# Two-layer hybrid attention and PEER kernel: rows summed twelve items late, query steps beside the lookups, the row's multiply ahead of the dense step

## What is computed

```python
q = (xc @ wq).reshape(P_CHUNK, P_HEADS, 2, P_HALF)
sc = jnp.einsum('thcd,hcnd->thcn', q, sub_keys)
s1, i1 = lax.top_k(sc[:, :, 0], P_TOPK)
s2, i2 = lax.top_k(sc[:, :, 1], P_TOPK)
# all 16 x 16 sums; the best 16 give top_s and eidx
...
gate = jax.nn.softmax(top_s, axis=-1)
u = jnp.take(u_tab, eidx, axis=0)
act = jax.nn.gelu(jnp.einsum('thkd,td->thk', u, xc))
vv = jnp.take(v_tab, eidx, axis=0)
return jnp.einsum('thk,thkd->td', gate * act, vv)
```

## Time and profile before

| | us |
|---|---|
| median of 3 runs | 3077.9 |
| lowest and highest run | 3075.38, 3078.37 |
| span of the profiled execution | 2949.8 |
| the median less that span | 128.1 |

### The profile page before, as it was taken

The page is one execution under the profiler, slowest core; times in us unless marked ns, Lnnn a source line. Parts: engine busy times, 40 slices in busy tenths (PEclk is TensorE's granted clock), DMA queues, the critical chain, the costliest instruction groups (busy, mean ns, idle before and its releaser), DMA issues.

```text
span 2949.8 us, 21918 instructions
## 1 busy us (share of the span) xinstructions
PE 1521.5 (52%) x6476; PEld 665.0 (23%) x6476; DVE 1618.3 (55%) x3970; ACT 280.5 (10%) x732; POOL 1562.8 (53%) x1601
## 2 busy tenths in 40 slices
PE   6677677677235523334445585776723333233344
PEld 2353235244001101111222133533500000000001
DVE  1427776454766556455641298655386675766510
ACT  0220023011000000001000002311100000000000
POOL 0006411376676556455566573126667777777765
PEclk9798775788557765566678896578866666556667
DMA  8669973699999989788899995248999999999988
GB/s 291 250 210 355 388 287 107 214 348 380 400 401 371 401 314 346 289 299 308 336 400 352 357 368 195 64 157 321 376 358 384 403 392 390 393 403 383 390 339 345
DMA packets 299015, 963.25 MB, mean 327 GB/s; under 512 B 28280, under 2 KB 30712, under 8 KB 298128
## 3 DMA queue, kind: packets, MB, share of 16 engines
q0 software_dynamic: 221184, 805.40, 71.4%
q1 hardware_dynamic: 77712, 156.44, 14.6%
HBM read 959.12 MB, written 2.62 MB: 326 GB/s over the span
## 4 chain that ended last, share of the span: by engine, by line
DMA 25%; PE 24%; DVE 17%; POOL 16%; issue 15%; ACT 1%; POOLq 0%; SPq 0%; DVEq 0%; ACTq 0%
DMA ring<-peer_v,v_rows 17%; POOL ring L670 16%; PE ps_acc L931 8%; DVE ring L1464 7%; DMA ring<-peer_u,u_rows 4%; PE ps_mm L754 3%; PE ps_mm L808 3%; DMA weights<-ada_w 2%; PE ps_mm L869 2%; DMA weights<-w_in 1%; PE ps_mb L834 1%; PE ps_acc L713 1%; PE ps_mm L897 1%; PE ps_tr L819 1%; PE ps_mb L693 1%
## 5 line engine op out<-in xcount | busy, mean ns | idle before, releaser
L931 PE MATMUL ps_acc<-ring,coef_cols 128*32 128x512 f32 x3072 | 603.9, 927 | 1137.7 <-DMA ring<-peer_v,v_rows 1137.7
L670 POOL DMA_INDIRECT ring<-peer_u,u_rows x768 | 785.9, 1023 | 668.2 <-DVE dots L1464 448.3
L670 POOL DMA_INDIRECT ring<-peer_v,v_rows x768 | 752.5, 980 | 444.6 <-issue 224.1
L1464 DVE CUSTOM_DVE_ANT_0 ring<-ring,ps_tr 128x1024 f32<-128x1024 f32 x512 | 616.3, 1220 | 330.0 <-DMA ring<-peer_u,u_rows 311.6
L931 PEld LDWEIGHTS ps_acc<-ring,coef_cols 128*32 128x32 f32 x3072 | 121.7, 145 | 1542.2 <-issue 1541.1
L1464 DVE CUSTOM_DVE_ANT_0 ring<-ring,h 128x1024 f32<-128x1024 f32 x256 | 307.7, 1224 | 111.7 <-DMA ring<-peer_u,u_rows 97.4
L754 PE MATMUL ps_mm<-weights,hT 128*128 128x512 f32 x480 | 218.1, 614 | 25.6 <-DMA weights<-w_in 21.1
L897 PE MATMUL ps_mm<-hT,weights 128*128 128x128 f32 (+1 forms) x1024 | 192.5, 345 | 3.6 <-issue 3.0
L897 PEld LDWEIGHTS ps_mm<-hT,weights 128*128 128x128 f32 x1024 | 164.3, 203 | 61.6 <-issue 48.0
L635 POOL TENSOR_SCALAR u_rows<-picks 128x16 uint32<-128x16 f32 x48 | 17.7, 368 | 230.8 <-DVE picks L1437 229.8
L1488 DVE TENSOR_TENSOR h<-h,ps_acc 128x1024 f32<-128x1024 f32 x6 | 7.3, 1221 | 224.3 <-PE ps_acc L931 224.3
(11 more groups left out here) (206 smaller groups left out, 1522.8 us busy)
## 6 DMA issues: line engine op xcount, KB each, us to landing
weights<-ada_w SPq DMA_DIRECT2D x24, 2048.0 KB, 9.9
weights<-w_in SPq DMA_DIRECT2D x20, 2048.0 KB, 14.3
weights<-peer_wq SPq DMA_DIRECT2D x16, 2048.0 KB, 13.8
weights<-w_out SPq DMA_DIRECT2D x8, 2048.0 KB, 15.6
ring<-peer_u,u_rows POOLq DMA_INDIRECT x768, 6.3
ring<-peer_v,v_rows POOLq DMA_INDIRECT x768, 6.4
weights<-peer_keys SPq DMA_DIRECT2D x4, 1024.0 KB, 6.5
par<-params SPq DMA_DIRECT2D x2, 1026.0 KB, 7.4
```

The lines of the kernel that those rows point to most:

```text
L670: pool.indirect_dma_start(ring[:, place % RING, :], None, src, bass.IndirectOffsetOnAxis(ap=rows, axis=0)).then_inc(row_full[place % RING] ...
L931: last = pe.matmul(ps_acc[QROWS * k:QROWS * (k + 1), b * NB:(b + 1) * NB], coef_cols[:, i // PART % 2, at:at + QROWS], ring[:, slot("v", n ...
L1464: dve.tensor_tensor_reduce(row, row, h, 1.0, 0.0, ALU.mult, ALU.add, dots[:, n // UNIT % 2, n % UNIT:n % UNIT + 1]).then_inc(u_used, 1)
```

## The change

It has four parts.

1. LAG is 12 instead of 8: TensorE adds v rows i - 15 to i - 12 at item i, and the last 12 behind the segment. ScalarE's third and fourth spread move from items 25 and 41 to 29 and 45. The order of lookups and the ring stay as they are.
2. Stages are cut into pieces. Of both stages of layer 0 and of the sample stage of layer 1 the first 5 pq steps stay with the stage, and 11 move beside the next lookups: the prompt's of layer 0 into unit 0 (weight 6 each), the sample's into the first 40 items of unit 2, those of layer 1 into the first 40 of unit 8. The prompt stage of layer 1 is as before. In layer 0 the sample stage's first 36 steps (through the 12th head of the first tile) go with unit 0, the rest up to the cut with unit 1; in layer 1 all up to the cut is spread evenly over units 6 and 7.
3. `route` waits for the two score copies of its own head instead of the stage's VectorE program waiting for all. The score matmuls of the sample stages go to `ps_mb` instead of `ps_tr`, and `hold_rows` no longer waits for the scores.
4. In an item with a u row VectorE makes its piece of the search, the gates and the multiply first, and the dense steps after them.

Cut to what differs:

```diff
-LAG = 8
+LAG = 12
...
+FIRST_PQ = 2 * AHEAD + 1
+def split_at(tiles):
+    return len(steps(tiles)) - 16 + FIRST_PQ
...
 class Beside:
-    def __init__(self, program, weights, weight, items):
-        self.program, self.weights, self.weight, self.share = program, weights, weight, weight / items
+    def __init__(self, pieces, programs, items):
+        self.steps = [(programs[piece.stage], weight) for piece in pieces for weight in piece.weights]
+        self.share = sum(weight for _, weight in self.steps) / items
...
     def item(self):
         self.due += self.share
-        while self.done < self.due - 1e-6 and self.done < self.weight:
-            self.done += self.weights[next(self.program)]
+        while self.at < len(self.steps) and self.done < self.due - 1e-6:
+            self.step()
...
+def pieces(name):
...
+    if name == "start":
+        return (Piece(P0, 0, split_at(P_TILES)),), 1
+    if name == "s0_first":
+        return (Piece(P0, split_at(P_TILES), None, 6), Piece(S0, 0, S0_HALF)), UNIT
+    if name == "s0_last":
+        return (Piece(S0, S0_HALF, split_at(S_TILES)),), UNIT
+    if name == "s0_rest":
+        return (Piece(S0, split_at(S_TILES)),), REST_ITEMS
+    if name == "p1":
+        return (Piece(P1),), 3 * UNIT + 20
+    if name == "s1":
+        return (Piece(S1, 0, split_at(S_TILES)),), 2 * UNIT
+    return (Piece(S1, split_at(S_TILES)),), REST_ITEMS
...
-    return (Segment(0, None, s0), Segment(1, 0, s0, True),
-            Segment(2, 1), Segment(3, 2, p1), Segment(4, 3, p1), Segment(5, 4, p1), Segment(None, 5, p1, True),
-            Segment(6, None, s1), Segment(7, 6, s1, True),
-            Segment(8, 7), Segment(9, 8), Segment(10, 9), Segment(11, 10), Segment(None, 11))
-SPREADS = {(0, S_TILES): 2 * UNIT, (1, P_TILES): 3 * UNIT + 20, (1, S_TILES): 2 * UNIT}
+    return (Segment(0, None, "s0_first", True), Segment(1, 0, "s0_last", True), Segment(2, 1, "s0_rest", True),
+            Segment(3, 2, "p1"), Segment(4, 3, "p1"), Segment(5, 4, "p1"), Segment(None, 5, "p1", True),
+            Segment(6, None, "s1"), Segment(7, 6, "s1", True), Segment(8, 7, "s1_rest", True),
+            Segment(9, 8), Segment(10, 9), Segment(11, 10), Segment(None, 11))
+REST_ITEMS = 40
+S0_HALF = 36
...
         def key_scores_at(l, tiles, i, n):
-            return ps_mb[:, (i % 2) * NB:(i % 2) * NB + n] if tight(l, tiles) else tr(i, n)
+            return tr(i, n) if (l, tiles) == P0 else ps_mb[:, (i % 2) * NB:(i % 2) * NB + n]
...
             def hold_rows(tau):
                 act.wait_ge(u_used, 2 * tau * UNIT)
-                act.wait_ge(ps_ready, group_nth(tau // T, S_TILES, 15, 16))
                 act.wait_ge(h_ready, nth(tau // T, S_TILES, 2, 2 * len(S_TILES) - 1))
...
                 for i in range(16):
                     yield "pq"
-                dve.wait_ge(ps_ready, group_nth(l, tiles, 15, 16))
...
             def route(n):
...
+                tiles = S_TILES if tau % T else P_TILES
+                dve.wait_ge(ps_ready, group_nth(tau // T, tiles, 2 * h + 1, 16))
                 dve.sem_inc(search_may, 1)
...
-                    side.item()
                     if g.u is None:
+                        side.item()
                         continue
...
                     dot(g.u * UNIT + i)
+                    side.item()
```

More of the change, by code:

```diff
@@ L129, in before_search, with __init__, step @@
         self.engine.sem_inc(self.search_may, 1)
[L132 to L137 removed]
+class Piece:
+    def __init__(self, stage, first=0, last=None, weight=None):
+        kinds = steps(stage[1])
+        weights = WEIGHTS[stage[1] == P_TILES]
+        self.stage = stage
+        self.weights = [weight or weights[kind] for kind in kinds[first:last]]
+class Beside:
+    def __init__(self, pieces, programs, items):
+        self.steps = [(programs[piece.stage], weight) for piece in pieces for weight in piece.weights]
+        self.share = sum(weight for _, weight in self.steps) / items
+        self.due, self.done, self.at = 0.0, 0, 0
+    def step(self):
+        program, weight = self.steps[self.at]
+        next(program)
+        self.done += weight
+        self.at += 1
     def item(self):
         self.due += self.share
[L141 to L142 removed]
+        while self.at < len(self.steps) and self.done < self.due - 1e-6:
+            self.step()
     def end(self):
[L145 to L151, removed]
+        while self.at < len(self.steps):
+            self.step()
 class Segment:
@@ L236, with stage_programs, program, start_beside @@
 PLACE = {which: n for n, which in enumerate(LOOKUPS)}
[L239 to L247, removed]
-                modulate(which)
-            yield w
-    return Beside(program(), WEIGHTS[tiles == P_TILES], dense_weight(tiles), SPREADS.get(of, UNIT))
+def stage_programs(modulate, dense_stages):
+    def program(stage):
+        for at, _ in enumerate(dense_stages(*stage)):
+            for which in PLAN.get(stage, {}).get(at, ()):
+                modulate(which)
+            yield
+    return {stage: program(stage) for stage in (P0, S0, P1, S1)}
+def start_beside(name, programs):
+    some, items = pieces(name)
+    return Beside(some, programs, items)
 def pair_of(i):
@@ L941, in _ @@
                 modulate(which)
-            start_beside((0, P_TILES), modulate, dense_stages).end()
-            side, of = nothing(), None
+            programs = stage_programs(modulate, dense_stages)
+            start_beside("start", programs).end()
+            side, of = start_beside(None, programs), None
             for g in segments():
@@ L1169, in _ @@
                     side.end()
-                    if g.u is not None:
+                    if g.u is not None and g.u % 2:
                         hold_rows((g.u + 1) // 2)
```

12 lines of the change are left out of this document (6 added, 6 removed).

## The result

The changed kernel took 2928.06 us (median of 4 runs, 2921.07 to 2933.83) against 3076.64 for the kernel before: ratio 0.9529, 95% interval 0.9503 to 0.9556, 149 us less by the medians. The forecast was 2968, in a range of 2905 to 3035. On a later occasion the same kernel had 0.9601 (0.9573 to 0.963, 123 us less by the ratio). On the later occasion one of the seven executions of the kernel before took 3335.21 us at a lower granted clock (0.526 instead of some 0.69) and does not count in the ratio.

The account below looks back on a forecast made before the run. The prediction took DMA transfers as the bound at 394 GB/s (2445 us), with about 505 us of stretches where the DMA engines lack work. Gains 60 + 8 + 28 + 14 = 110 off the 3077.9 median gave 2968 us, range 2905 to 3035.

Parts of the forecast that it names:

- 128.1 us lie around the span: Whole kernel: the median of 3077.9 us exceeds the profiled span of 2949.8 by time around it, untouched by the change.
- The rule on HBM: Prompt stage of layer 1: the skill's limit of about 358 GB/s would make the gain 44 us instead of 60.
- The lag in the prompt stage: Prompt stage of layer 1: LAG 12 and the earlier multiply shorten waits; 60 us gained, bounds 15 and 77.
- No VectorE wait over 5 us: Sign of being right, prompt stage: no VectorE wait of over 5 us for TensorE's scores, windows of 370 GB/s and more.
- GpSimd's issue: Lookups: GpSimd's issue takes 1.02 us against 1.33 us for a lookup, so it can keep up with the transfers.
- The order within an item: Prompt stage of layer 1: the multiply ahead of the dense step gives one more item, 2.7 us, at no instruction cost.
- The start: First stage: search begins some 24 us earlier, first lookup near 193 us; net 8 us gained, bounds 0 and 20.
- Sample stage, layer 0: Units 0 to 2: unit 1 ends at 670 instead of 711 us; 28 us gained of its own, bounds 0 and 60.
- Query steps in unit 2: Layer 0's moved sample query steps: hidden with a TensorE margin of 2.5 us; the last query block costs 5 us.
- Sample stage, layer 1: Units 6 to 8: stage ends at 2111 against 2130 us; less 5 for the late block, 14 gained, bounds -15 and 45.
- Slower: v slots come free too late: Rival: GpSimd waits for TensorE's adds; at 1.5 us lost in each of 112 groups, 3136 us; chance 0.07.
- the sample chains eat their share: Rival: multiplies and adds lengthen the sample chains; only start and prompt stage pay, 68 us, so 3010; chance 0.13.

Follow-up runs that it names:

- lag12_dotfirst: The kernel before with LAG 12 and VectorE's multiply ahead of the dense steps, the stages uncut: 2967.8 us, ratio 0.9642.
- after_again: The changed kernel itself, unchanged, run again on a later occasion: 2954.32 us, ratio 0.9601 to the kernel before.
- base_again: The kernel before, unchanged, one execution profiled again: span 3062.7 us, time 3064.47 us.
- second profile of before: The trace of the kernel before, unchanged, taken after the result: span 3062.7 us in an execution of 3064.47 us.
- first profile: The trace of the kernel before, unchanged, that the prediction was made from: span 2949.8 us.

## Why the prediction was right, and where it was not

- **Direction and size.** Forecast 110 us less, measured 149 and 123. The main reason, TensorE's late adds, was right and the sum low. That the sum came so near is partly luck, because two terms were off in opposite directions. The lag with the order was priced at 60 and gave 110 alone (lag12_dotfirst). The pieces were priced at 50, and behind the lag they gave 13 us on the same occasion (2954.32 against 2967.8, with intervals that overlap) and 35 by the ratio of the first occasion; without the lag they cost 51.
- **Where the pieces pay and cost.** Between the traces of lag12_dotfirst and after_again, which differ by the pieces alone, 16 us are gained up to the end of unit 1 and 25 in units 6 and 7. The moved query steps take 9 of these back in unit 2 (206 instead of 197) and 11 in unit 8 (200 instead of 189). The prediction had 5 us for each.
- **The span.** The step "128.1 us lie around the span" failed: it is 1.8 us (base_again). All rates in the prediction (394 GB/s, 1.33 us for a lookup, 505 us of stretches with too little to do) are of one execution with fast lookups. At the 362 GB/s of the others 963.25 MB take 2661 us, and of a span of 3062.7 about 402 were such stretches. A second profile or the spans of other runs would have told, and the 128 us should have made me ask. The wrong step did not move the forecast, since the sum was taken off the median; it did enter the terms that were worked out at 385 or 394 GB/s, and no run separates by how much.
- **The rule on HBM.** In all traces of this case but one the pure lookups ran at 352 to 363 GB/s (2450 to 2600 us), and I had set the rule aside with rows of the one at 393 to 395. The Trainium skill, "DMA: Bandwidth & Descriptors", section "Where 436 GB/s comes from", names about 358 GB/s per core. The pure lookups of most traces lie near that figure, but it is no bound here: the page of the changed kernel, above, has 403 and 407 GB/s in its 14th and 22nd slice, where blocks of weights share the DMA engines with the lookups, and the second profile of before has 408 in its 22nd. By the rule's rate the gain in the prompt stage was to be 44 us; measured were 59.
- **The lag in the prompt stage.** 60 forecast, 59 measured for all parts together (table), 63 for the lag alone. The mechanism was right, and the size of this stage too. "No VectorE wait over 5 us" was a bit too strong (6.4), GpSimd's long waits for VectorE are fewer but not gone (up to 9.1 us), and the windows reach 342 to 373 GB/s, not 370 and more. What the term left out is the lag's gain outside this stage, some 40 of its 104 us.
- **GpSimd's issue.** The prediction took 1.02 us for it. But it also stands idle for 0.30 us between two issues (time line of the first profile from 2500 us on: 0.94 us of work and 0.30 idle, a lookup each 1.24 us), so beside a lookup of 1.33 us its margin is small.
- **The order within an item.** Priced at one item, together with the lag. Alone it gave 64 us, behind the lag 6 to 15. That the two overlap was right; the size alone was not.
- **The start.** The first lookup is issued at 189.32 us (forecast 193, before 216.66). Of the 24 us I let 8 stay; the runs allow 0 to 15.
- **Sample stage, layer 0.** Forecast 508, 584, 606, 670 for the start and end of the output projection, the first query step and the end of unit 1; the time line has 522, 592, 629, 679. The first tile and the chain behind it took 14 us more than I said, norm and keys 37 instead of 22. The output projection took 70 instead of 76. And 17 of the 29 us gained by the end of unit 1 come with the lag alone, which ended it at 691.
- **Query steps in unit 2.** I costed them at a late block (5 us), hidden by TensorE's margin of 2.5 us. Unit 2 took 206 us instead of the 196 with the lag alone. Windows of unit 2 with the lag alone and in the changed kernel, and a piece of the latter's time line:

```profile
691.00:887.00 196.00, 56.91 (x265) 11.82 (x263) 126.53 (x337) 5.93 (x18) 125.56 (x136) 0.59 0.99 373
```

```profile
679.00:885.00 206.00, 102.15 (x482) 53.35 (x482) 125.39 (x337) 13.29 (x38) 122.39 (x133) 0.71 0.97 368
```

```profile
727.43 0.49 DVE L1441 MAX8 half_top<-scores 128x8 f32<-128x128 f32 x2 [12.04 <-ACT scores L1119]
...
730.16 0.94 POOL L708 DMA_INDIRECT ring<-peer_u,u_rows  x1 [6.49 <-DVE dots L1504]
```

  TensorE is busy for 102 instead of 57 us. VectorE comes to the search of the third head before its score copies are there and stands for 12 us, as the prediction did not look at how early a search needs its step. The first five query steps cover two heads and half of the third, whose search begins at item 8; behind it GpSimd stands for 6.49. So the hidden steps cost some 5 us more than said.
- **Sample stage, layer 1.** 14 forecast (19 to the end of unit 7), 36 measured. The chain to the output projection took 192 us, not 172, but it started at 1721 instead of at a place 30 us later than before: unit 6's first multiply to the last input projection took 93 us in the changed kernel and 86 before, not 112. That was the mis-sized term: I had the projections end with the 64th multiply, but TensorE adds no v rows there and runs ahead: its last projection ended at 1721, the last multiply of unit 6 at 1753.
- **Not in the sum:** 13 us between the last multiply of unit 5 and the first of unit 6. With the order alone this stretch was 139 us, with the lag alone 153, before 148: it comes with the order, which lets the first multiplies go ahead of the sample stage's norms; some of it is only where the mark is set.
- **The rivals.** "Slower: v slots come free too late" is shown to exist, at LAG 16. The rival "the sample chains eat their share" was half right. In layer 0 the chain from the last input projection to the output projection grew from 178 to 184 us and held 22 lookups instead of 24, so the new spread gained nothing in it. In layer 1 it grew from 160 to 192 us and held 57 instead of 24.

## What to carry to other kernels

Where one engine takes both rows that arrive late and steps that another engine waits for, its order of work is a coupling: compare, in the order of the transfers, the row that it waits for with the row that its partner could already use, and move the late row's work back by that many items, but not past the point where its slots are needed again. Price such edits together: here one part was worth 104 us alone, another 64, both 110, and a third cost 51 without the first and gave 13 to 35 behind it. A sum can come out near the measured time while its terms do not, so each term needs its own run. And before a trace is used as a yardstick, hold its span against the times of other runs.

## What the runs showed of the hardware

The same kernel with the same bytes ran its pure lookups at 396 GB/s in one execution and at 362 in another (2250 to 2450 us of both profiles of before), and its span moved from 2949.8 to 3062.7 us. In the twelve other traces units 9 to 11, the same work in all, took 559 to 571 us (568 in the second profile, 513 in the first). The granted TensorE clock doesn't tell the two apart: it was 0.710 and 0.691 on average over the span, and the changed kernel had 0.708 with its lookups at 353. No run here tells what does.

The lower figure is one of lookups alone, not of the DMA engines. In the changed kernel's execution the slices with pure lookups (the 32nd to 38th) have 340 to 363 GB/s and the 22nd, with weights beside them, 407. Why lookups alone stay below that is open.
